# Seven block products in place of eight for four of the 22 K-tile pairs of the feed-forward output matrices

## What is computed

```python
FFN_HIDDEN = 5632
# first block
gate, up = jnp.split(h @ w_ffn_in[l], 2, axis=-1)
x = x + rms_norm((jax.nn.silu(gate) * up) @ w_ffn_out[l], ffn_post_g[l])
# second block
def swiglu(h, w_in, w_out):
    z = h @ w_in
    a, b = z[..., :D_FF], z[..., D_FF:]
    return (jax.nn.silu(a) * b) @ w_out
h = h + swiglu(rmsnorm(h, ffn_norm_g[i]), ffn_w_in[i], ffn_w_out[i])
return rmsnorm(h, final_norm_g)
```

## Time and profile before

| what | value |
|---|---|
| median of 3 runs | 2426.8 us (2426.61 to 2428.27) |
| profiled execution, own time | 2427.59 us |
| its span, first to last instruction | 2425.3 us |
| TensorE busy | 2406.8 us, 99% of the span |
| VectorE busy | 1673.4 us, 69% |
| ScalarE busy | 1304.1 us, 54% |
| mean granted TensorE clock | 0.999 |
| stage `fo1` on TensorE | 1051.2 to 1292.0 us |
| stage `fo2` on TensorE | about 2177.5 to 2418 us |

### The profile page before, as it was taken

One profiled execution on the slowest core, in us unless ns is written; L12 is line 12 of the kernel. 1 busy time (PEld: TensorE's weight loads), 2 busy tenths in 40 slices (PEclk: granted clock), 3 DMA queues, 4 the chain that ended last, 5 costly groups with the idle time before them and its releaser, 6 DMA issues.

```text
span 2425.3 us, 33378 instructions
## 1 busy us (share of the span) xinstructions
PE 2406.8 (99%) x12195; PEld 2008.9 (83%) x12195; DVE 1673.4 (69%) x2305; ACT 1304.1 (54%) x1813; POOL 36.9 (2%) x60
## 2 busy tenths in 40 slices
PE   9999999999999999999999999999999999999998
PEld 7888888897888888888887889998788888888887
DVE  5568888677888888864446536777788888884444
ACT  5665558665555555544445435554655555554443
POOL 1000000000000000000000010000000000000000
PEclk9999999999999999999999999999999999999999
DMA  7765545545556555666656775435565565656554
GB/s 236 241 207 187 161 149 176 165 158 170 178 191 223 190 193 182 199 223 195 194 192 204 218 223 157 145 109 157 159 203 192 190 216 190 196 194 214 193 191 156
DMA packets 233853, 455.82 MB, mean 188 GB/s; under 512 B 16698, under 2 KB 19002, under 8 KB 233232
## 3 DMA queue, kind: packets, MB, share of 16 engines
q1 hardware_dynamic: 227008, 431.49, 55.6%
q0 software_dynamic: 6160, 21.81, 2.6%
q10 hardware_dynamic: 576, 1.05, 0.1%
HBM read 449.04 MB, written 5.24 MB: 187 GB/s over the span
## 4 chain that ended last, share of the span: by engine, by line
PE 93%; DVE 3%; ACT 1%; DMA 1%; issue 1%; DVEq 0%; SPq 0%; ACTq 0%
PE g L320 12%; PE g L321 12%; PE g L322 12%; PE g L1173 9%; PE g L1175 9%; PE g L1174 9%; PE g L1577 4%; PE g L1579 4%; PE g L1578 4%; PE m L1136 1%; PE m L1138 1%; PE m L1137 1%; PE g L2514 1%; PE g L2518 1%; PE g L2516 1%; PE g L1136 1%
## 5 line engine op out<-in xcount | busy, mean ns | idle before, releaser
L308 DVE TENSOR_TENSOR wl<-raw,wh 128x1024 fp32r<-128x1024 f32 (+1 forms) x820 | 991.0, 1219 | 591.4 <-ACT wh L304 578.2
L304 ACT ACTIVATE wh<-raw 128x1024 fp32r<-128x1024 f32 (+1 forms) x819 | 858.5, 1055 | 867.2 <-PE g L322 395.3
L1173 PE MATMUL g<-wh,act_hi 128*128 128x512 f32 x960 | 374.8, 390 | 0.4 <-DVE shared L1355 0.4
L1175 PE MATMUL g<-wh,act_lo 128*128 128x512 f32 x960 | 373.5, 389 | 0.0
L1174 PE MATMUL g<-wl,act_hi 128*128 128x512 f32 x960 | 373.5, 389 | 0.0
L320 PE MATMUL g<-wh,ht_hi 128*128 128x512 f32 x672 | 261.6, 389 | 0.0
L322 PE MATMUL g<-wh,ht_lo 128*128 128x512 f32 x672 | 261.4, 389 | 0.0
L321 PE MATMUL g<-wl,ht_hi 128*128 128x512 f32 x672 | 261.4, 389 | 0.0
L1173 PEld LDWEIGHTS g<-wh,act_hi 128*128 128x128 f32 x960 | 180.2, 188 | 38.5 <-issue 0.8
L1175 PEld LDWEIGHTS g<-wh,act_lo 128*128 128x128 f32 x960 | 180.2, 188 | 37.7
L1174 PEld LDWEIGHTS g<-wl,act_hi 128*128 128x128 f32 x960 | 180.2, 188 | 37.2
(11 more groups left out here) (476 smaller groups left out, 3550.9 us busy)
## 6 DMA issues: line engine op xcount, KB each, us to landing
raw<-in_w_ffn_in SPq DMA_DIRECT2D x176, 512.0 KB, 4.4
raw<-in_ffn_w_in SPq DMA_DIRECT2D x176, 512.0 KB, 4.4
raw<-in_w_in SPq DMA_DIRECT2D x111, 512.0 KB, 4.5
raw<-in_w_ffn_out SPq DMA_DIRECT2D x88, 512.0 KB, 4.4
raw<-in_ffn_w_out SPq DMA_DIRECT2D x88, 512.0 KB, 3.8
raw<-in_nsa_w_in SPq DMA_DIRECT2D x80, 512.0 KB, 4.4
raw<-in_w_out SPq DMA_DIRECT2D x32, 512.0 KB, 4.4
raw<-in_nsa_w_out SPq DMA_DIRECT2D x32, 512.0 KB, 4.8
```

The costliest lines, as they stand in the source:

```text
L304: nc.scalar.activation(wh[:, j % SLOTS, 0:n], raw[:, j % SLOTS, 0:n], ACT.Copy).then_inc(hi_done, 1)
L308: nc.vector.tensor_tensor(wl[:, j % SLOTS, 0:n], raw[:, j % SLOTS, 0:n], wh[:, j % SLOTS, 0:n].bitcast(F32), ALU.subtract).then_inc(lo_don ...
L1173: nc.tensor.matmul(dst, h, whk, start=(t in starts and k == 0), stop=False)
L1175: ins = nc.tensor.matmul(dst, l, whk, start=False, stop=(last and k == 1))
```

## The change

In `fo1` and `fo2` the four column chunks are taken as two pairs. For K-tile pairs 0 to 3 (`FO_K = 4`) both chunks of a pair are done together by one seven; pairs 4 to 21 stay units of 12 matmuls, first those of the even chunk, with the sevens among them, then the 18 of the odd chunk. `FO_GAPS` says how many units stand ahead of each seven and behind the last: 9, 3, 2, 2, 2 for the first pair of chunks, 5, 4, 3, 3, 3 for the second. A stage then has 104 slot uses in place of 88 units. The sums of activation blocks are made on VectorE behind units 3 and 6 (`dve_sums_of_x`), the shared terms are formed behind the third unit after the last seven of a pair of chunks (`up_rows`) and added by `rows_into`: in `fo1` to the finished chunk in PSUM, in `fo2` to `x`, at once for both chunks. In `fo1` the last chunk's shared terms are subtracted row tile by row tile at the border (`fold`), and ScalarE's square waits for that.

```diff
+FO_K = 4
+FO_GAPS = ((9, 3, 2, 2, 2), (5, 4, 3, 3, 3))
+def out_order():
+    order = []
+    for p, gaps in enumerate(FO_GAPS):
+        units = list(range(FO_K, FKT // 2))
+        left = iter(units)
+        for b, gap in enumerate(gaps):
+            order += [("unit", 2 * p, next(left), 0) for _ in range(gap)]
+            if b < FO_K:
+                order += [("seven", p, b, q) for q in range(4)]
+        order += [("unit", 2 * p + 1, u, 0) for u in units]
+    return order
...
             def square(t):
-                act.wait_ge(*((tile_used, SKEWED[name]) if t == 0 else (unit_used, used(s, c))))
+                if name == "fo1":
+                    act.wait_ge(ff_step, fo_stepped(name, 1, FO_STEP["rest"] + t))
+                else:
+                    act.wait_ge(*((tile_used, SKEWED[name]) if t == 0 else (unit_used, used(s, c))))
...
+            def fold(t):
+                dve.wait_ge(*((tile_used, SKEWED[name]) if t == 0 else (unit_used, used(s, c))))
+                nc.vector.tensor_tensor(g[:, 2 + t, :], g[:, 2 + t, :], fo_rest[1][:, t, :], ALU.subtract).then_inc(ff_step, 1)
+                dve.wait_ge(ff_step, fo_stepped(name, 1, FO_STEP["rest"] + t))
+
             def variance(t):
+                if name == "fo1":
+                    fold(t)
...
+        def sp_out(sp, name):
+            for n, (kind, c, u, q) in enumerate(OUT):
+                if kind == "unit" and n - SLOTS not in OUT_AT:
+                    sp_unit(sp, cyc, n, columns(c, u))
+                if kind == "seven" and q == 1:
+                    sp_unit(sp, cyc, n, columns(2 * c + 1, u))
+                    sp_behind(sp, cyc, n + 3, columns(*OUT[n + 3][1:3]))
+                if n + 1 in OUT_AT:
+                    sp.dma_start(raw[:, SLOTS, :].rearrange("p (k n) -> p k n", k=2), columns(2 * OUT[n + 1][1], OUT[n + 1][2]))\
+                      .then_inc(ahead_in, 16)
...
+        def dve_out(dve, name, evac, turned_from):
+            def up_rows(p):
+                dve.wait_ge(ff_kept, fo_m1_kept(name, p))
+                dve.wait_ge(unit_used, SLOTS + s["u0"] + OUT_AT[FO_K * p + FO_K - 1] + 4)
+                nc.vector.tensor_tensor(fo_step[:, :], kept[:, 0, :], m[:, 3, :], ALU.add).then_inc(ff_step, 1)
+                dve.wait_ge(ff_step, fo_stepped(name, p, FO_STEP["u2"]))
+                nc.vector.tensor_tensor(kept[:, 1, :], fo_step[:, :], m[:, 1, :], ALU.add).then_inc(ff_step, 1)
+                dve.wait_ge(ff_step, fo_stepped(name, p, FO_STEP["u3"]))
+                nc.vector.tensor_tensor(rest[p][:, 0, :], fo_step[:, :], m[:, 2, :], ALU.add)
+                nc.vector.tensor_tensor(rest[p][:, 1, :], kept[:, 1, :], m[:, 2, :], ALU.add).then_inc(ff_step, 1)
+                dve.wait_ge(ff_step, fo_stepped(name, p, FO_STEP["up"]))
...
+                if n - 6 in OUT_AT and OUT[n - 6][2] == FO_K - 1:
+                    p = OUT[n - 6][1]
+                    up_rows(p)
+                    if name == "fo2":
+                        for c in range(2):
+                            rows_into(p, c, x[:, :, (2 * p + c) * NB:(2 * p + c + 1) * NB])
...
-            pe_gemm(pe, "fo1", ht_hi, ht_lo, also={2: lambda: pe_ff_turn(pe, "ff1", PAIRS - 1),
-                                                   20: lambda: turned_in(pe, "ff1", 2 * PAIRS)}, skew=True,
-                    between=lambda: [pe_part_turn(pe, "n2", 0, part) for part in range(3)])
+            pe_out(pe, "fo1", "ff1")
+            pe_last_units(pe, "fo1", ht_hi, ht_lo, lambda: [pe_part_turn(pe, "n2", 0, part) for part in range(3)])
```

More of the change, by code:

```diff
@@ L38 @@
 FKT = FH // P
+FO_K = 4
[11 more added lines that the diff above has]
+    return order
+OUT = out_order()
+OUT_END = [max(n for n, o in enumerate(OUT) if o[0] == "unit" and o[1] == c) for c in range(4)]
+OUT_AT = [n for n, o in enumerate(OUT) if o[0] == "seven" and o[3] == 0]
 KV = F_HG
@@ L280, in build @@
             else:
-                at_unit += FF_UNITS if name in ("ff1", "ff2") else s["units"] * s["chunks"]
+                at_unit += {"ff1": FF_UNITS, "ff2": FF_UNITS, "fo1": len(OUT), "fo2": len(OUT)}.get(name, s["units"] * s["chunks"])
                 at_pair = [at_pair[0] + (s["chunks"] + 1) // 2, at_pair[1] + s["chunks"] // 2]
@@ L325, in used @@
         def used(s, chunk):
+            if s in (gemms["fo1"], gemms["fo2"]):
+                return SLOTS + s["u0"] + OUT_END[chunk] + 1
             return SLOTS + s["u0"] + s["units"] * (chunk + 1)
@@ new lines, in pe_seven, with product, of_x, converted @@
+        def pe_seven(pe, cyc, j, hi, lo, k0, sums_of, first, last, up_free):
+            def product(q, half, rows, dst, start, stop):
+                slot = (j + q) % SLOTS
+                whk, wlk = wh[:, slot, half * NB:(half + 1) * NB], wl[:, slot, half * NB:(half + 1) * NB]
+                nc.tensor.matmul(dst, rows[0], whk, start=start, stop=False)
+                nc.tensor.matmul(dst, rows[0], wlk, start=False, stop=False)
+                return nc.tensor.matmul(dst, rows[1], whk, start=False, stop=stop)
+            def of_x(k, t):
+                return [b[:, k0 + k, t * P:(t + 1) * P] for b in (hi, lo)]
+            def converted(q):
+                pe.wait_ge(lo_done, SLOTS + (cyc + (j + q) // SLOTS) * SLOTS + (j + q) % SLOTS + 1)
+            converted(0)
+            product(0, 0, of_x(0, 0), m[:, 0, :], first, last)
+            product(0, 1, of_x(1, 0), g[:, 0, :], False, False).then_inc(unit_used, 1)
+            converted(1)
+            if first:
+                pe.wait_ge(pair_free[1], up_free)
+            product(1, 1, sums_of(3), g[:, 2, :], first, False).then_inc(unit_used, 1)
+            converted(2)
+            product(2, 0, sums_of(2), m[:, 1, :], first, last)
+            product(2, 1, sums_of(0), m[:, 2, :], first, last).then_inc(unit_used, 1)
+            converted(3)
+            product(3, 0, sums_of(1), m[:, 3, :], first, last)
+            product(3, 1, of_x(1, 1), g[:, 1, :], False, False).then_inc(unit_used, 1)
@@ new lines, in dve_sums_of_x @@
+        def dve_sums_of_x(dve, hi, lo, k0, whole, sums):
+            tiles = [b[:, k0:k0 + 4, :].bitcast(F32).rearrange("p (s k) (t n) -> p s k t n", s=2, t=T) for b in (hi, lo)]
+            link_d(dve, nc.vector.tensor_tensor(whole[:, :, :, :, :], tiles[0], tiles[1], ALU.add))
+            a11, a12, a21, a22 = (whole[:, :, k, t, :] for t in range(T) for k in range(2))
+            link_d(dve, nc.vector.tensor_tensor(sums[:, :, 0, :], a22, a21, ALU.subtract))
+            nc.vector.tensor_tensor(sums[:, :, 2, :], a11, a21, ALU.subtract)
+            link_d(dve, nc.vector.scalar_tensor_tensor(out=sums[:, :, 1, :], in0=sums[:, :, 0, :], scalar=-1.0, in1=a11,
+                                                       op0=ALU.mult, op1=ALU.subtract))
+            nc.vector.tensor_tensor(sums[:, :, 3, :], a12, sums[:, :, 1, :], ALU.add).then_inc(ff_summed, 1)
```

301 lines of the change are left out of this document (180 added, 121 removed).

## The result

The changed kernel takes 2438.3 us in the median of 5 runs (2436.6 to 2441.7), the kernel before 2426.8 (5 runs, 2426.3 to 2428.3). The ratio is 1.0048, with a 95% interval of 1.0033 to 1.0063: 11.5 us slower, where 3.4 us faster was forecast. The runs also spread by 5 us, where they spread by 2 us before.

What follows compares the result with a forecast made beforehand. TensorE, busy 99% of the span, was taken as the bound. Terms -10.9 + 3.0 + 2.8 + 1.7 = -3.4 us took 2427.6 to 2424.2, median expected 2423.4; range of 8 in 10, 2419 to 2428.

Steps and rivals of the forecast that it cites:

- Price of a matmul, 48 fewer: In `fo1` and `fo2`, 48 matmuls removed at 0.2267 us each: -10.9 us.
- Gaps of two units: First pair's third and fourth sevens wait for q0, 0.6 and 0.95 us: 1.5 us a stage, 3.0 us in all.
- I take 4.2: Time in us from issue of q1's load to VectorE's weight sums, used in the timetable of sevens.
- Gaps of three units: At sevens three units apart, the round ends at S + 12.15, due S + 12.92: hidden, no cost.
- its slower rival: VectorE loses its lead in gaps of three too, at landings of some 5 us: +6 us, 2432.8 us, chance 0.05.
- Shared terms and `x`: Behind last sevens: hidden in `fo1`; in `fo2` the next conversion 1.8 and 1.0 us late, together 2.8 us.
- The border: Behind `fo1`, tile 1's subtraction and ScalarE's square delay `x` and TensorE's transposes: 1.7 us, between 0 and 1.7.
- Average load is no bound: VectorE's 6.8 us under a seven's 4.76 is repaid, barely, by two units leaving 1.5 us each; latency may bound.
- The bounds of the terms: Costs at other landings: gaps of two 1.1 to 5.9 us, shared terms with additions to `x` 1.7 to 4.5 us.
- its slower end: Slow end of the 8 in 10 range: 2428 us, at a landing of 4.7 us.

Runs made afterwards that it cites:

- The half loads: Changed kernel with each out-stage seven's two own loads (load ahead and q1's) moving half their columns, 256 KB for 512: 2425.7 us, ratio 0.9999.
- the second trace of the changed kernel: Trace of the changed kernel run again, unedited, beside some of the follow-up runs: 2436.7 us, ratio 1.0046 to the kernel before.
- without the subtraction: Changed kernel without the shared terms' subtraction at the border behind `fo1` and ScalarE's wait for it: 2435.1 us, ratio 1.0046.
- other gaps: Changed kernel with 7, 3, 3, 3, 2 units for 9, 3, 2, 2, 2 in the first pair of chunks: 2442.2 us, ratio 1.0071.
- short sums: Changed kernel with the second and third weight sum of each out-stage seven adding 64 columns for 512: 2428.0 us, ratio 1.0010.
- the additions moved away: Changed kernel with the `fo2` additions to `x` behind the 9th and 13th slot after the last seven's start: 2432.5 us, ratio 1.0024.
- two, three and four mended sevens: Changed kernel, that many sevens per pair, later `x` additions, border reordered: two 2420.5 us; three 2421.2, or 2419.2 with load ahead first; four, load ahead first, 2427.2.

## Why the prediction was wrong

- **Price of a matmul, 48 fewer: right.** The distance of 0.227 us stayed.
- **Gaps of two units: right place, wrong size,** 6.1 us for 3.0. The failing term is "I take 4.2" from issue to the sums. The slot came free at S + 2.8 (3.0 forecast), and 3.9 us of sums and conversion were right; the landing was 5.15, the term 5.3. The 4.2 came from medians of loads in a steady stream of units. A seven breaks this stream: its slots come free together, no load runs for some 3.5 us (the last one lands at 1099.57, the next is issued at 1103.02), and then the load ahead, q1's, the one behind and the units' leave within 2 to 4 us. The row of 4.4 us for q1's load in `ff1` had a gap of four or more before it. The half loads show the effect from the other side.
- **Gaps of three units: "Hidden with 0.7 us to spare" was wrong,** 2.8 us in the change and 0.6 to 1.6 per seven where they come in a row. The forecast named this as its slower rival, with landing beyond 5 us, and gave it 5% because no median was near 5. The median is indeed no measure: for units and q1 together it rose only to 4.8 and 4.6 us in `fo1` (3.7 and 4.5 before), and it is q1's load, late in its burst, at 4.6 to 6.5 us that decides.
- **Shared terms and `x`: right place, wrong size,** 6.9 us for 2.8 (and 0.49 in `fo1` for none). VectorE's instructions took what they were priced at. The third unit's load took 6.04 us for 4.2 behind the eighth seven, and that seven was itself late by 1.5, which the forecast excluded ("not late, so q2 is 0.7 to 0.9 earlier").
- **The clock: not foreseen,** 1.7 us in the first trace, some 5.4 in the second. The prediction put it at nothing, without a reason.
- **The border: right,** 1.5 for 1.7; half of it can be had back by another order.
- **Average load is no bound: right.** VectorE's idle time in `fo1` is still 75 of 224 us.
- Of the rest of 3.9 us, 1.1 lies ahead of `fo1`, where the change does nothing but shift the program's lines and data. It is a difference between executions: 0.8 of it is waits at sevens of `ff1`, and in the second trace of the changed kernel `fo1` began at 1049.3, 1.8 us earlier than before the change. The small distances in the out stages aren't explained.
- **The bounds of the terms don't come out.** By the prediction's own timetable the gaps of two cost 0, 4.2 and 5.0 us at landings of 3.5, 4.5 and 4.7, where it has 1.1, 5.1 and 5.9, and the shared terms with `x` at most 1.4, 3.4 and 3.8, where it has 1.7, 4.3 and 4.5. The forecast at 4.2 doesn't hang on them; its slower end does, and right sums would put it lower still, further from what was measured.

The formula of the Trainium skill (SBUF — State Buffer, "The DMA setup-cost knee") gives 3.2 us for such a load, an estimate, of which 1.20 us are its 512 KB at the 436 GB/s of that section. The traces of the out stages have no load that quick: the quickest took 3.5 us, q1's and those behind it in a burst 4.6 to 7.3. The 1.20 us come near to the 1.25 to 1.35 between two landings in a full queue.

## What to carry to other kernels

When an edit lets several buffers come free at once, don't price the next load by the median of a steady stream: count the loads that leave within its landing time, and take its landing from a load that stands in such a burst (here 4.6 to 6.5 us for q1's, against 3.7 in the quickest window of the steady stream). Adding the 1.25 to 1.35 us between queued landings for each load ahead is no rule: with three ahead it would give 7.6 us (3.7 and three times 1.3), where 5.62 was measured. Check then the whole round, from a buffer's release to the engine's next need, against the work between; a round that is too long by 1 us is paid at every seven, since a late one leaves the next no lead. And cheap work of VectorE goes where the bound engine has a lead, not right behind the place at which the lead is smallest: three small reorderings and half to three quarters of the edit here beat the whole edit, by 16 to 17 us.

## What the runs showed of the hardware

- Loads of 512 KB that are issued 0.4 to 2 us apart land 1.25 to 1.35 us apart in most pairs behind the second of a burst, up to 2 in some. The first of a burst keeps its time, and the second loses most: behind the fourth seven of `fo1` the load issued at 1115.13 took 3.73 us, and those at 1116.27, 1117.41 and 1118.66 took 5.54, 5.93 and 5.93; between the first two landings lie 2.95 us.
- Halved loads (q1's, 256 KB) landed after 2.9 us in the median of each out stage, although whole ones stood beside them.
- TensorE's granted clock fell to half, and came back after some 7 to 9 matmuls (twice after some 14), around standstills of 3.37 us in the changed kernel's first trace, 1.89, 3.10 and 3.06 in its second, 2.52 and 3.05 with half loads, 2.02 without the subtraction and, with other gaps, the 1.29 at the border (1294.80). It didn't fall behind standstills of 2.33 us in that first trace (2258.80), 2.99 with short sums and 2.65 without the subtraction. So the length of one standstill doesn't decide. In the run with the additions moved away (longest standstill 1.94 us), and in those with two, three and four mended sevens, it fell in neither out stage.
